# Fifty-seven delta-rule steps packed into the first iterations of an attention loop, with the gated norm two iterations earlier

## The reference, cut to what matters

```
def token_mixing(x, fox_cache, page_table, conv_buf, S0, mix):
    ...
    if fox_cache is None:
        o_a = fox_prompt(qa, ka, va, logf)
        o_g, S = gdn_chunked(qg, kg, vg, g, beta, S0)
    else:
        cache_k, cache_v, cache_logf = fox_cache
        o_a = fox_sample(qa, ka, va, logf, cache_k, cache_v, cache_logf, page_table)
        o_g, S = gdn_recurrent(qg, kg, vg, g, beta, S0)
    o_g = rmsnorm(o_g.astype(x.dtype), g_gdn) * jax.nn.silu(z.reshape(B, T, GDN_HEADS, GDN_HEAD_DIM))
    y_a = o_a.reshape(B, T, FOX_WIDTH) @ w_branch_fox
    y_g = o_g.reshape(B, T, GDN_WIDTH) @ w_branch_gdn
    y = (jax.nn.sigmoid(gate_a) * y_a + jax.nn.sigmoid(gate_b) * y_g) @ w_out
```

## Time and profile before

| what | us |
|---|---|
| median of 3 runs | 1643.65 (1642.38 to 1644.22) |
| the profiled execution's own time | 1641.8 |
| its span, first to last instruction | 1640.0 |
| PE busy | 1525.7 (93%) |
| DVE, ACT, POOL busy | 602.3, 500.6, 131.0 |
| mean granted PE clock, as a share of full speed | 0.967 |
| the loop over t: first `scores` to the last `low` | 852.8 to 1096.2 |

### The profile page before, as it was taken

The page is one execution under the profiler, slowest core; times in us unless marked ns, Lnnn a source line. Parts: engine busy times, 40 slices in busy tenths (PEclk is TensorE's granted clock), DMA queues, the critical chain, the costliest instruction groups (busy, mean ns, idle before and its releaser), DMA issues. The chain is left out here.

```text
span 1640.0 us, 31045 instructions
## 1 busy us (share of the span) xinstructions
PE 1525.7 (93%) x12584; PEld 1395.7 (85%) x12584; DVE 602.3 (37%) x902; ACT 500.6 (31%) x741; POOL 131.0 (8%) x152
## 2 busy tenths in 40 slices
PE   5999999899788999999988999979979999998995
PEld 4999999899686788887866887759969999998995
DVE  3333333211433656223257533346253333332113
ACT  4222222222422246322123333243353222222221
POOL 0000000000044000222210220011000000000000
PEclk8999999999888999999999999989989999999998
DMA  3222223222067997999986757936212222232221
GB/s 108 90 92 93 97 90 103 72 89 83 27 212 221 393 312 256 351 337 330 371 310 230 268 167 254 305 111 221 78 39 77 92 97 92 90 99 72 88 88 52
DMA packets 111938, 268.75 MB, mean 164 GB/s; under 512 B 15401, under 2 KB 15914, under 8 KB 111090
## 3 DMA queue, kind: packets, MB, share of 16 engines
q1 hardware_dynamic: 105586, 244.25, 43.1%
q0 software_dynamic: 6272, 23.34, 3.9%
HBM read 253.29 MB, written 14.26 MB: 163 GB/s over the span
## 5 line engine op out<-in xcount | busy, mean ns | idle before, releaser
L130 DVE TENSOR_TENSOR w_low<-w_raw,w_high 128x1024 fp32r<-128x1024 f32 (+1 forms) x180 | 232.9, 1296 | 766.4 <-ACT w_high L126 743.7
L126 ACT ACTIVATE w_high<-w_raw 128x1024 fp32r<-128x1024 f32 (+1 forms) x180 | 200.6, 1116 | 760.5 <-PE psum L151 727.0
L147 PE MATMUL psum<-h_high,w_high 128*128 128x260 f32 x1408 | 287.0, 285 | 14.9 <-DVE h_low L227 14.9
L151 PE MATMUL psum<-h_high,w_low 128*128 128x260 f32 x1408 | 285.7, 285 | 0.0
L149 PE MATMUL psum<-h_low,w_high 128*128 128x260 f32 x1408 | 285.2, 284 | 0.0
L147 PEld LDWEIGHTS psum<-h_high,w_high 128*128 128x128 f32 x1408 | 219.0, 190 | 16.7 <-issue 14.4
L151 PEld LDWEIGHTS psum<-h_high,w_low 128*128 128x128 f32 x1408 | 219.0, 190 | 0.0
L149 PEld LDWEIGHTS psum<-h_low,w_high 128*128 128x128 f32 x1408 | 218.5, 190 | 0.0
L147 PE MATMUL psum<-mix_h_high,w_high 128*128 128x260 f32 x704 | 149.3, 294 | 8.0 <-DVE mix_h_low L227 6.6
L147 PE MATMUL psum<-a_high,w_high 128*128 128x260 f32 x704 | 146.7, 290 | 10.4 <-DVE a_low L383 10.4
L149 PE MATMUL psum<-mix_h_low,w_high 128*128 128x260 f32 x704 | 144.1, 287 | 0.0
(11 more groups left out here) (309 smaller groups left out, 1752.9 us busy)
## 6 DMA issues: line engine op xcount, KB each, us to landing
kv_ring<-in_cache_k SPq DMA_DIRECT2D x256, 256.0 KB
kv_ring<-in_cache_v SPq DMA_DIRECT2D x256, 256.0 KB
w_raw<-in_w_gu SPq DMA_DIRECT2D x88, 512.0 KB
w_raw<-in_w_dn SPq DMA_DIRECT2D x32, 704.0 KB
w_raw<-in_w_proj SPq DMA_DIRECT2D x44, 512.0 KB
spill<-h_f POOLq DMA_DIRECT2D x20, 260.0 KB
gates<-spill POOLq DMA_DIRECT2D x16, 260.0 KB, 3.4
w_raw<-in_w_merge SPq DMA_DIRECT2D x8, 512.0 KB
```

The lines of the kernel that those rows point to most:

```text
L126: act.activation(w_high[:, u, 0:nk, :], w_raw[:, u, 0:nk, :], ACT.Copy).then_inc(high_done, 1)
L130: dve.tensor_tensor(w_low[:, u, 0:nk, :], w_raw[:, u, 0:nk, :], w_high[:, u, 0:nk, :].bitcast(F32), ALU.subtract).then_inc(low_done, 1)
L147: pe.matmul(out[h], w_high[:, u, k, :], high[:, k0 + j, tok[h]], start=s, stop=False)
L151: mm = pe.matmul(out[h], w_low[:, u, k, :], high[:, k0 + j, tok[h]], start=False, stop=e)
```

## The change

Two things move; no instruction of the computation is added or left out.

1. `step_at` spreads over `len(steps)` = 57 places instead of 62. So step n stands at place n: the iterations 0 to 27 hold two steps each, and iteration 28 the last `update` in its first half.
2. The gated norm's parts are tied to GATED = N - 3 = 29 instead of 31. The squares, the first sums and logarithms and POOL's product stand in iteration 29, the rest of the sums and logarithms and the exponentials in iteration 30, DVE's product and the rounding in iteration 31. DVE's low parts (L1574 before), which stood behind the loop, stand in iteration 32, ahead of `out_scaled(30)`. In ACT's list the copy of the sample output (L1116) stays in iteration 33.

```diff
@@ core
+            GATED = N - 3
@@ step_at
-                n, places = 2 * t + half, 2 * (N - 1)
+                n, places = 2 * t + half, len(steps)
@@ gpsimd: zt * cv
-                        if t == N - 1:
+                        if t == GATED:
@@ scalar: squares, gated_log(0), (1); gated_log(2), (3) and Exp; gdn_high
-                        if t == N - 1:
+                        if t == GATED:
-                        if t == N:
+                        if t == GATED + 1:
+                        if t == GATED + 2:
                             for h in range(GH):
                                 act.wait_ge(z_dve, h + 1)
@@ vector
-                        if t == N + 1:
+                        if t == GATED + 2:
                             for h in range(GH):
                                 dve.wait_ge(z_inv, h // 2 + 1)
                                 dve.wait_ge(z_pool, h + 1)
...
+                        if t == GATED + 3:
+                            for h in range(GH):
+                                dve.wait_ge(z_high, h + 1)
+                                dve.tensor_tensor(gdn_low[:, h, :], cv[:, h, :], gdn_high[:, h, :].bitcast(F32),
+                                                  ALU.subtract).then_inc(z_low, 1)
...
-                    for h in range(GH):
-                        dve.wait_ge(z_high, h + 1)
-                        dve.tensor_tensor(gdn_low[:, h, :], cv[:, h, :], gdn_high[:, h, :].bitcast(F32),
-                                          ALU.subtract).then_inc(z_low, 1)
                     low(3)
```

## The result

The changed kernel is slower: a median of 1651.59 us (1647.47 to 1653.12, 4 runs) against 1643.37 (1642.38 to 1644.22, 4 runs) for the kernel before, a ratio of 1.0052 with a 95% interval from 1.0040 to 1.0065. That is +8.2 us. The forecast had the sign right and the size wrong: +3.8 us. The measured median lies at the very end of its range, 1651.6.

A forecast was written before the change was run, and what follows sets the result against it. PE's list bounds the loop's middle, waits on other engines its head, ACT and DVE latencies its end. +6.8 + 1.2 - 6.4 + 2.2 = +3.8 us, giving a 1647.4 us median; range 1641.6 to 1651.6.

The forecast's parts named there:

- Part 1: Loop's middle: four steps move ahead of `scores(29)`, which therefore starts 6.8 us later.
- `scores(29)` starts at about 1070: Expected sign in the changed profile for the last tiles; later than 1073 would count as wrong.
- what this takes from the iterations 29 and 30 comes back in part 3: Loop's end: time of the steps removed from these iterations is regained behind `scores(29)`, within the -6.4 us.
- the walk: Hand-carried engine timeline; for the end it gave 34.07 us for the measured 34.1 in the old order, trusted to about 1 us.
- Part 2: Loop's head, iterations 0 to 5: steps move up half an iteration, +1.2 us more waiting, bounds -8.7 and +4.4, range -1 to +3.
- A wait for cache pages on PE: Loop's middle: seeing such a wait in the changed profile would show the forecast wrong; no size given.
- Part 3: From `scores(29)` to the loop's end: 27.7 us against 34.1, 6.4 less, supposing PE at 2.4 GHz.
- DVE's four products ... follow POOL to 18.6: Loop's end: DVE's products, 2.77 us in all, start at 14.7 and end at 18.6 us behind the start of `scores(29)`.
- The clock, +2.2: Loop's end: after idling, PE runs its last pieces at 1.2 GHz, costing 2.2 us; bounds 0 and 3.
- The rival in which the clock holds: Loop's end: PE keeps full clock, or the head costs nothing; +1.6 us, 1645.2; chance 0.27.
- The rival with the drain: ACT's table switches in the end: each holds ACT 1.38 us longer; +6.6 us, 1650.2; chance 0.04.
- a z that lands 3 us late: Loop's end: late z moves POOL's and DVE's products and all behind by 3 us; +6.8, 1650.4; chance 0.12.

The follow-up runs named there:

- e1: Against the kernel before: only the steps moved to 57 places, the norm left where it was; ratio 1.0035.
- b0: The kernel before, unchanged, profiled once more in a single execution; loop 245.2 us, no ratio.
- e5: Against the changed kernel: places 0 and 12 (first halves of iterations 0 and 6) left empty again; ratio 1.0026 to the kernel before.
- e2: Against the changed kernel: only place 0, the first half of iteration 0, left empty again; ratio 1.0034 to the kernel before.
- e4: Against the changed kernel: DVE waits for all four of POOL's products before its own; single execution, loop 251.5 us, no ratio.
- e11: Against the changed kernel: unread PE products added, 2 ahead of `probs_turned(31)` and 10 ahead of `out_columns(1)`; ratio 1.0037 to the kernel before.
- e10: The changed kernel itself, measured a third time; ratio 1.0050 to the kernel before.
- e9: Against the changed kernel: unread PE products added, 2 ahead of `probs_turned(31)` and 5 ahead of `out_columns(1)`; ratio 1.0051 to the kernel before.
- e8: Against the changed kernel: places 0 and 12 empty, z by POOL's queue, the end reordered by when inputs come; ratio 0.9988 to the kernel before.
- e3: Against the changed kernel: SP loads z ahead of the merge's two weight blocks; ratio 1.0030 to the kernel before.

## Why the prediction was right or wrong

**Part 1, the moved steps, +6.8: right in size.** The sign "`scores(29)` starts at about 1070" held (1070.62), but only because the loop began 1.6 us earlier in this execution. Counted from the loop's start, `scores(29)` comes 10.1 us later in this pair of profiles: 6.7 for the moved steps and 3.4 for the head, below. But the step "what this takes from the iterations 29 and 30 comes back in part 3" was true of the walk and not free: with the steps alone moved (e1) it came back short by the wait of 1.7 us for value pages, and the stretch behind `scores(31)` stayed as it was.

**Part 2, the head, +1.2: the larger of the two steps that failed.** The step is "Carrying PE, DVE and ACT forward by hand ... I get 1.2 us more waiting". It measured +3.4 in this pair, beyond the +3 of its bounds, and +2.2 in the others against b0, so 1.0 to 2.2 more than forecast; in waits it is +3.0 in this pair and +1.3 to +2.6 over the others. The walk named the right place: `spread(3)` behind `turn(2)` in iteration 4. But it gave `raw`, `turn` and `spread` together too little (9.5 to 11.4 us, +1.9 in this pair). And it left out a queue: the `key_pair` of iteration 5 moved behind the wait of `raw(3)`, so the time between it and the `key_pair` that needs its place in the ring fell from 12.5 to 10.4 us, and PE waited 1.1 us at 906.95. A wait for cache pages on PE was what the text named as a sign that it was wrong. e5 clears both waits at once; e2, with its own new ones, shows that the first place alone isn't enough.

**Part 3, the end, -6.4 at full clock: mis-sized by 1.5, the other step that failed.** ACT's list came as walked: the norm's last exponential ended at 1085.91, 15.3 us behind the first instruction of `scores(29)` (1070.62), for 15.6; the exponential of tile 31 followed at once. z landed 12.9 us behind it, the figure that the text has, but by luck: the text's own terms (-0.6 + 4.5 + 8.6) make 12.5, and SP issued z 5.1 us behind the value pair instead of 4.5 (1075.07 behind 1069.98). DVE's first product started at 14.4 for 14.7. The step that failed is "DVE's four products ... follow POOL to 18.6": they ended at 1090.72, thus at 20.1. It took POOL's 5.00 and DVE's 0.75 each from rows in which the two didn't meet (POOL was done at 1081.54, DVE began at 1090.09). The very point of the change, an earlier product, made them meet. All behind it moved by 1.4 to 1.7 us (`masked(1)` ended at 23.0 for 21.6, the loop at 31.6 for 27.7 + 2.2 = 29.9), and e4 shows that the two durations are back when they are kept apart. The Trainium skill, SBUF — State Buffer, section SBUF: two separate sides, says that GpSimd and a VectorE operation with two inputs in SBUF share a pair of ports as an exclusive lock, so that the later one blocks for the whole instruction of the other; by the alternation above the trace agrees, and `z * cv` and L1562 both read two tensors in SBUF.

**The clock, +2.2: right, and in its parts too.** 2.22 us by e11 against e10, as 0.9, 0.9 and 0.5 where the text has 0.85, 0.9 and 0.5. The rival in which the clock holds is out: 0.50 from 1088 on. e11 adds to e9 only five more products, which fill PE's idle time ahead of `out_columns`: with that idle time the stretch behind stands at 0.50, without it at 1.00.

**The table loads.** Four, each 1.28 us, and each followed by its operation within 0.02 us (L1114 at 1083.88 behind 1082.58 + 1.28). The rival with the drain is out for this kernel.

**The sum.** The forecast's terms make +3.8; the measured ones 6.7 + 3.4 - 2.5 = +7.6, the growth of the loop. The medians grew by 8.2. The miss of 4.4 us is, by this pair, the head (2.2), the end (1.7, of which 1.5 is the meeting of POOL and DVE), and 0.6 between this one execution and the medians, less 0.1 in part 1. That 1651.59 still touches the end of the range is luck: its +8 was made of a z that lands 3 us late and a walk that is 1 us off, and z wasn't late.

The change's idea fails for a plain reason: the middle of the loop is full on PE, so steps moved into it move everything behind them, and the five empty places weren't idle time. They gave other engines their time, and with them filled PE waits elsewhere.

## What to carry to other kernels

Before you fill a gap in a hand-written order, ask which wait it covers on this engine and which buffer the instructions behind it free; an empty place on a busy engine costs nothing. When a change brings two engines' work together for the first time, the durations of the rows in which they ran apart are lower bounds, above all for POOL beside a DVE operation that reads two tensors. In the end of a loop order each engine's list by when its inputs come, and let nothing that only the output needs stand ahead of the chain that ends last: that won 5.5 us of tail here (e5 30.7, e8 25.2), against 2.5 for the change.

## What the runs showed of the hardware that I had not expected

- POOL and DVE take turns when both read two tensors in SBUF: a product of 128x520 rises from 1.25 to 1.75 us on POOL and from 0.75 to 1.79 on DVE, with little won by overlap (7.2 us for the eight, and 4 x 1.25 + 4 x 0.75 is 8.0).
- The clock at the loop's start differs between executions of one program. In the earlier trace rows it is 0.50 at 854 to 856 and the view has 1.00 from 860 to 864; in b0, the same kernel, it fell a second time (below). So it did in all twelve later executions, and in neither of the first pair, before and after:

```profile
860.00:864.00 4.00, 4.00 (x28) 3.71 (x32) 2.20 (x6) 0.56 (x2) 0.00 (x0) 0.60 0.86 294
```

  With the same places `scores(4)` starts at 29.2 and 31.4 us (before), and at 31.9 (after) to 33.5 us in the eight with the change's places. What makes the clock fall again was not settled, nor whether it goes with the chip, since each profile is one execution. A comparison of single profiles of this loop is good to some 2 us in the head, and to 0.1 to 1 us in the tail.
- The same transfer of z, issued by SP behind two weight blocks, took 8.2 to 10.1 us from issue to landing in eleven executions (6.8 in e3, ahead of those blocks), and in e11 that hid half of what the clock gave.
